# Low parts of the weights behind four attention stages made by GpSimd instead of VectorE

## The chip, the core and the metric

The kernel runs on one core of a Trainium2 chip, as one program. The metric is the device time of one execution in microseconds. Five engines work side by side, each with its own in-order queue, and meet by semaphores: TensorE (PE) multiplies matrices, VectorE (DVE) and ScalarE (ACT) work elementwise, GpSimd (POOL) is a fourth compute engine that the kernel before leaves idle, and SyncE (SP) issues the transfers of the weights.

## What is computed

Two transformer blocks over 256 tokens of width 2048, in float32, batch 1. The first has a sliding-window attention with grouped keys, relative bias and sinks, a gated linear attention in chunks of 64, gates, and a SwiGLU feed-forward net of width 5632. The second has a short causal convolution, a latent attention (MLA, 16 heads, low-rank queries and keys, rotary part, RMS norm per head), an attention over 256 memory tokens, three gates and an output product. Cut to what matters here:

```python
u = rmsnorm(h); proj = u @ w_in                      # 2048 x 8720, then split
ya = sliding_window_attention(qa, ka, va, sinks, rel_bias) @ w_proj_a
ob = gated_linear_attention(qb, kb, vb, log_a)
merged = sigmoid(gate_a) * ya + sigmoid(gate_b) * ((rmsnorm(ob) * silu(ob_gate)) @ w_proj_b)
h = h + merged @ w_out; h = h + (silu(z @ w_gate) * (z @ w_up)) @ w_down; x = rmsnorm(h)
# second block
proj = rms_norm(x) @ w_in_2                          # then split
q = rms_norm(c_q) @ w_uq; kv = rms_norm(c_kv) @ w_ukv    # per head: norm, rope, softmax, product
merged = sigmoid(g_conv)*o_conv + sigmoid(g_mla)*o_mla + sigmoid(g_mem)*o_mem
x = x + merged @ w_o
```

Nearly all the arithmetic is activations (256 rows) times weights; all weights are read once, 460 MB.

## The kernel before

A product of float32 values is made of three matmuls in a reduced float32 format (fp32r): each operand x is held as a high part (x rounded to fp32r) and a low part (x minus that), and the product is hi*hi + hi*lo + lo*hi.

The weights stream in granules of at most 1024 columns on 128 partitions (two blocks of 128 rows by 512 columns as a rule). `segments()` lists all chunks in the one order in which every engine walks them; `ALL` is the flat list. 866 granules go through two rings: `raw` with RAW = 8 slots and `w_hi`/`w_lo` with SPL = 4 slots. Per granule:

- SP loads a raw slot (L386), after `lo_done` shows that its last content was used up (the wait stands right before it).
- ACT makes the high part with a copy (L963), after the transfer landed and after TensorE used the ring slot (`w_used`), and increments `hi_done`.
- DVE makes the low part by a subtraction (L1270) after `hi_done`, and increments `lo_done`.
- PE waits for `lo_done` and runs 12 matmuls of 512 columns (L437 to L439), then increments `w_used`.

ACT and DVE also do everything else: norms, softmax, gates, copies out of PSUM. The order on each engine is written out by hand. A class `Walk`, one instance for ACT and one for DVE, keeps count and issues splits (high parts on ACT, low parts on DVE) at chosen places: `ahead(n)` issues n; `split_next`, `some` and `more` issue those of the next chunk; `background(...)` with `back(k)` serves the attention stages.

In an attention stage PE alternates between a "unit" (a group of small matmuls or transposes into a PSUM bank, `unit(fill)`, which waits for `unit_src` from DVE) and `back(k)`, k granules of a background chunk. While PE works on these, DVE and ACT prepare the next unit. `W.back(k)` on ACT and DVE first fills the ring to four granules ahead and then goes on with the attention's own instructions; so on DVE the low parts stand in line before them. ACT's counterpart runs its high parts at the same places of its own queue, each as soon as PE frees a slot, and waits for `act_req` only before its exponentials.

The four stages and what streams behind them: the window attention (`qb, kb, vb, vb, glow, ob, ob`), the gated linear attention (three each of `gate_a, proj_a`), the attention over the memory (`ge`, 4 chunks), and MLA, a loop of 2 turns with 4 pairs of heads each. A pair runs `uq` and `ukv`, its own products, and behind its attention `mz` (even pairs) or `gc` and `conv_out` (odd pairs). In a pair DVE copies the two results out of PSUM (L2140, L2147, L2150), runs `W.back`, then the norm chain: 12 sums of squares (L1284), `rsqrt` as 11 dependent instructions on 12 columns (L1290 to L1299), the scaled queries (L2172, releases the first unit), the rotary part (L2179, L2090 to L2098, released at L2184), the scaled keys (L2189). In the memory stage the like chain ends at L1958 and L1961. Both chains work from SBUF to SBUF.

Of the kernel before, what the change touches and what calls it, by code (L numbers as in the profile page):

```python
# [29 lines left out]
ALU = mybir.AluOpType  # L30
# [56 lines left out]

GRAN = 1024
RAW, SPL = 8, 4
BIASW = 384  # L90


# [22 lines left out]
def bias_constants():  # L115

    dist = 255 - np.arange(BIASW)
    d = np.maximum(dist, 0)
# [3 lines left out]
    onehot = ((np.arange(NB)[:, None] == bucket[None, :]) & seen[None, :]).astype(np.float32)  # L122
    mask = np.broadcast_to(np.where(seen, 0.0, NEG).astype(np.float32), (AH, BIASW))
    return onehot, np.ascontiguousarray(mask)
# [6 lines left out]
class Count:  # L131
# [10 lines left out]
    def next(self, by=1):  # L142
        self.n += by
        return self.at()
# [24 lines left out]
def need(eng, sem, value):  # L169

    if isinstance(value, int) and value <= 0:
        return
    eng.wait_ge(sem, value)
# [73 lines left out]
def build(nc, ap, out, scratch):  # L247
    SEG = segments()
    ALL = [(c, k) for _, n, cs in SEG for k in range(n) for c in cs]

    with ExitStack() as ctx:
        def sb(name, shape, dt=F32):
            return ctx.enter_context(nc.sbuf_tensor(name, shape, dt))

        def sem(name):
            return ctx.enter_context(nc.semaphore(name))


        raw = sb("raw", [P, RAW, GRAN])
        w_hi = sb("w_hi", [P, SPL, GRAN], F32R)  # L260
        w_lo = sb("w_lo", [P, SPL, GRAN], F32R)
        w_hi32 = w_hi[:].bitcast(F32)
# [22 lines left out]
        def area(kb, nkb):  # L285
            return arena[:, int(kb * 256):int((kb + nkb) * 256)]
# [6 lines left out]
        qb = area(30, 4).rearrange("p (t n) -> p t n", t=T)  # L293
        kb = area(34, 4).rearrange("p (t n) -> p t n", t=T)
        vb = area(38, 8).rearrange("p (t n) -> p t n", t=T)
        ob = area(46, 8).rearrange("p (t n) -> p t n", t=T)
# [10 lines left out]
        gtmp = work[:, 0:1024].rearrange("p (t n) -> p t n", t=T)  # L307
        bias_row = work[0:AH, 0:BIASW]
        onehot = work[0:NB, 512:512 + BIASW]
        rel_b = work[0:NB, 1024:1024 + AH]  # L310
        bmask = work[0:AH, 1536:1536 + BIASW]
        merged1 = area(22, 16).rearrange("p (k t n) -> p k t n", k=4, t=T)
# [35 lines left out]


        landed = [sem(f"landed{i}") for i in range(RAW)]  # L350
        hi_done, lo_done = sem("hi_done"), sem("lo_done")
        w_used = sem("w_used")
        acc_free = sem("acc_free")
        unit_src, unit_done, unit_free = sem("unit_src"), sem("unit_done"), sem("unit_free")
# [10 lines left out]
        block = ctx.enter_context(nc.Block())  # L365

        def weight_src(c, g, i):
            w = ap[c.weight]
            col = c.col if c.step == 0 else c.col + i * c.step
            v = w.rearrange("(k p) n -> p k n", p=P)[:, g * c.per:(g + 1) * c.per, :]  # L370
            return v[:, :, bass.ds(col, c.w)]


        @block.sync
        def _(sp):
            sp.dma_start(xres[:], ap["x"].rearrange("(t p) n -> p t n", p=P)).then_inc(x_in, 16)
            G = Count()
            for name, n, chunks in SEG:
                def granule(dst_size, src, shape):

                    need(sp, lo_done, G.at(1 - RAW))
                    s = G.slot(RAW)
                    dst = raw[:, s, 0:dst_size]
                    if shape > 1:
                        dst = dst.rearrange("p (k n) -> p k n", k=shape)
                    sp.dma_start(dst, src).then_inc(landed[s], 16)  # L386
                    G.n += 1

                def body(i):
                    for c in chunks:  # L390
                        if c.name == "ffn_down":
                            for k in range(8):
                                src = ap["w_ffn_down"].rearrange("(k p) n -> p k n", p=P)
                                src = src[:, bass.ds(i * 4 + k // 2, 1), (k % 2) * 1024:(k % 2 + 1) * 1024]
                                granule(GRAN, src.rearrange("p a n -> p (a n)"), 1)
                        else:
                            for g in range(c.grans):
                                granule(c.per * c.w, weight_src(c, g, i), c.per)

                if n <= 2:  # L400
                    for i in range(n):
                        body(i)
                else:
                    per = 8 if name == "ffn_down" else sum(c.grans for c in chunks)
                    with engine_loop(sp, n, {G: per}) as i:
                        body(i)
                if name == "kva":

                    sp.wait_ge(b_ready, 16)
                    shifted = bass.AP(scratch.tensor, P - 1, [[BIASW, P], [P * (BIASW + 1), AH], [1, 2 * P]])  # L410
                    sp.dma_start(bias_t, shifted).then_inc(b_ready, 16)
            for k in range(D // CW):
                sp.wait_ge(out_ready, k + 1)
                sp.dma_start(out.rearrange("(t p) n -> p t n", p=P)[:, :, k * CW:(k + 1) * CW],
                             xres[:, :, k * CW:(k + 1) * CW]).then_inc(stored, 16)
            sp.wait_ge(stored, 16 * (D // CW))
# [3 lines left out]
        def _(pe):  # L420
            G, C, U, XS = Count(), Count(), Count(), Count()
            mm = pe.matmul

            def granule(c, g, bank, banks_of=None):

                pe.wait_ge(lo_done, G.at(1))
                s = G.slot(SPL)
                per, w = c.per, c.w
                hi = w_hi[:, s, 0:per * w].rearrange("p (k n) -> p k n", k=per)
                lo = w_lo[:, s, 0:per * w].rearrange("p (k n) -> p k n", k=per)  # L430
                for k in range(per):
                    kt = g * per + k
                    for t in range(T):
                        xh = XH[c.x][:, c.x0 + kt, t * P:(t + 1) * P]
                        xl = XL[c.x][:, c.x0 + kt, t * P:(t + 1) * P]
                        o = acc[bank][:, t, 0:w]
                        mm(o, xh, hi[:, k, :], start=(kt == 0), stop=False)  # L437
                        mm(o, xh, lo[:, k, :], start=False, stop=False)  # L438
                        last = mm(o, xl, hi[:, k, :], start=False, stop=(kt == c.kts - 1))  # L439
                last.then_inc(w_used, 1)  # L440
                G.n += 1
# [220 lines left out]
            n, chunks = next((n, cc) for nm, n, cc in SEG if nm == "ffn_up")  # L662
# [18 lines left out]
            def down(first, last_pass):  # L681
                for k in range(4):

                    if k == 0:
                        XS.n += 1
                        pe.wait_ge(x_split, XS.at(0))
                    for half in range(2):
                        pe.wait_ge(lo_done, G.at(1))
                        s = G.slot(SPL)
                        for t in range(T):  # L690
                            xh = XH["A"][:, par4(k), t * P:(t + 1) * P]
                            xl = XL["A"][:, par4(k), t * P:(t + 1) * P]
                            for q in range(2):
                                o = DG[t * 4 + half * 2 + q]
                                a, z = w_hi[:, s, q * 512:(q + 1) * 512], w_lo[:, s, q * 512:(q + 1) * 512]
                                f = first and k == 0
                                e = last_pass and k == 3
                                mm(o, xh, a, start=f, stop=False, skip_group_check=True)  # L698
                                mm(o, xh, z, start=False, stop=False, skip_group_check=True)  # L699
                                last = mm(o, xl, a, start=False, stop=e, skip_group_check=True)  # L700
                        last.then_inc(w_used, 1)
                        G.n += 1
# [3 lines left out]
            def par4(k):  # L706
                return par[0] * 4 + k
            down(True, False)
            par[0] = 1
            down(False, False)  # L710
# [79 lines left out]
            n, chunks = next((n, cc) for nm, n, cc in SEG if nm == "mla")  # L790
# [466 lines left out]
            plain(4)  # L1257


        @block.vector  # L1260
        def _(dve):
            W = Walk(dve)
# [3 lines left out]

            def split(n):
                s, r = W.G.slot(SPL), W.G.slot(RAW)
                dve.wait_ge(hi_done, W.G.at(1))
                dve.tensor_tensor(w_lo[:, s, 0:n], raw[:, r, 0:n], w_hi32[:, s, 0:n], ALU.subtract).then_inc(lo_done, 1)  # L1270
                W.G.n += 1
            W.split = split

# [552 lines left out]
            n = FF // CW  # L1826
# [475 lines left out]
```

## Time and profile before

| | us |
|---|---|
| runs, median of three (lowest, highest) | 2821.07 (2819.31, 2821.19) |
| the profiled execution | 2820.21 |
| its span from first to last instruction | 2818.4 |
| PE busy | 2639.2 (94%) |
| DVE busy | 1618.3 (57%) |
| ACT busy | 1067.8 (38%) |
| POOL busy | 0.2 (0%) |

A row of the windows gives for a stretch of the span the busy time of each engine with its instructions, then the granted clock of TensorE as a share of full speed, the busy share of the DMA engines and GB/s. A row of the waits gives who waited, at which line, for which engine and line, the sum in us, how often, and the longest. A row of the timeline gives the start and length in us, engine, line, instruction, what it writes and reads, and in brackets the idle time before it with what ended it; rows with x2 or x4 are instructions in succession, merged. The ends of matmuls are modelled, and they overlap, so a gap between two matmuls reads a little shorter than it is.

### The profile page before, as it was taken

How to read it: one execution, taken by the hardware profiler on the slowest of the kernel's cores; microseconds unless marked ns; L12 is line 12 of the kernel's file. 1: busy time of each engine (PE TensorE's matmuls, PEld its weight loads, DVE VectorE, ACT ScalarE, POOL GpSimd, SP SyncE). 2: the span in 40 equal slices, each digit the busy share in tenths (PEclk: the TensorE clock that was granted, in tenths of full speed). 3: DMA queues.
4: the chain of work that ended last, by engine and by line, in shares of the span. 5: the costliest groups of instructions: out<-in, count | busy, mean ns of one | idle time of the engine just before them, and what ended most of it. 6: DMA issues, size and time to landing. Idle time of an engine off the chain costs nothing.

```text
span 2818.4 us, 32577 instructions
## 1 busy us (share of the span) xinstructions
PE 2639.2 (94%) x11795; PEld 2158.8 (77%) x11795; DVE 1618.3 (57%) x2531; ACT 1067.8 (38%) x1245; POOL 0.2 (0%) x4
## 2 busy tenths in 40 slices
PE   5999889999999999989987899999997998999999
PEld 4778666888888888878875678788886777777887
DVE  5564555456655555555566754545666776765554
ACT  3333422444443434434443334334333332334443
POOL 0000000000000000000000000000000000000000
PEclk9998999999999999999998899999998999999999
DMA  5853434655666666645563355466543443445554
GB/s 187 220 158 113 127 119 135 194 179 194 187 188 192 182 196 188 190 158 195 192 219 120 112 164 165 145 180 190 179 153 107 151 146 126 134 148 174 190 186 138
DMA packets 235264, 466.56 MB, mean 166 GB/s; under 512 B 19035, under 2 KB 27505, under 8 KB 234498
## 3 DMA queue, kind: packets, MB, share of 16 engines
q1 hardware_dynamic: 231296, 457.89, 51.9%
q10 hardware_dynamic: 3842, 7.01, 1.3%
q8 instruction: 77, 1.26, 0.2%
q14 instruction: 49, 0.40, 0.0%
HBM read 459.60 MB, written 5.24 MB: 165 GB/s over the span
## 4 chain that ended last, share of the span: by engine, by line
PE 85%; DVE 9%; DMA 2%; issue 2%; ACT 1%; DVEq 0%; SPq 0%; ACTq 0%
PE acc L437 24%; PE acc L439 23%; PE acc L438 23%; PE banks L496 2%; DVE w_lo L1270 1%; PE acc L698 1%; PE banks L699 1%; PE acc L699 1%; PE banks L700 1%; PE acc L700 1%; PE banks L698 1%; DMA bias_rows<-work 1%; DVE etmp L1284 1%; ACT w_hi L963 1%; DMA raw<-in_w_in_dram 1%
## 5 line engine op out<-in xcount | busy, mean ns | idle before, releaser
L1270 DVE TENSOR_TENSOR w_lo<-raw,w_hi 128x1024 fp32r<-128x1024 f32 (+2 forms) x866 | 1044.6, 1218 | 919.7 <-ACT w_hi L963 897.6
L963 ACT ACTIVATE w_hi<-raw 128x1024 fp32r<-128x1024 f32 (+2 forms) x866 | 909.8, 1055 | 1425.0 <-PE acc L439 1265.6
L437 PE MATMUL acc<-w_hi,x_hi_A 128*128 128x512 f32 (+2 forms) x1824 | 730.3, 400 | 21.9 <-DVE w_lo L1270 14.3
L439 PE MATMUL acc<-w_hi,x_lo_A 128*128 128x512 f32 (+2 forms) x1824 | 716.7, 393 | 0.0
L438 PE MATMUL acc<-w_lo,x_hi_A 128*128 128x512 f32 (+2 forms) x1824 | 716.3, 393 | 0.0
L437 PE MATMUL acc<-w_hi,x_hi_B 128*128 128x512 f32 (+1 forms) x1344 | 530.7, 395 | 19.7 <-DVE w_lo L1270 15.2
L438 PE MATMUL acc<-w_lo,x_hi_B 128*128 128x512 f32 (+1 forms) x1344 | 525.6, 391 | 0.0
L439 PE MATMUL acc<-w_hi,x_lo_B 128*128 128x512 f32 (+1 forms) x1344 | 525.3, 391 | 0.0
L437 PEld LDWEIGHTS acc<-w_hi,x_hi_A 128*128 128x128 f32 x1824 | 355.1, 195 | 101.6 <-issue 17.7
L439 PEld LDWEIGHTS acc<-w_hi,x_lo_A 128*128 128x128 f32 x1824 | 354.1, 194 | 72.5
L438 PEld LDWEIGHTS acc<-w_lo,x_hi_A 128*128 128x128 f32 x1824 | 355.4, 195 | 69.2 <-issue 0.8
L437 PEld LDWEIGHTS acc<-w_hi,x_hi_B 128*128 128x128 f32 x1344 | 256.7, 191 | 73.4 <-DVE w_lo L1270 16.2
L439 PEld LDWEIGHTS acc<-w_hi,x_lo_B 128*128 128x128 f32 x1344 | 256.1, 191 | 51.4
L438 PEld LDWEIGHTS acc<-w_lo,x_hi_B 128*128 128x128 f32 x1344 | 256.5, 191 | 49.6
L496 PE MATMUL banks<-cst,stage 128*128 128x128 f32 (+1 forms) x429 | 77.7, 320 | 104.1 <-DVE stage L1375 33.7
L496 PEld LDWEIGHTS banks<-cst,stage 128*128 128x128 f32 (+1 forms) x429 | 57.5, 161 | 125.3 <-DVE stage L1375 40.3
L698 PE MATMUL acc<-w_hi,x_hi_A 128*128 128x512 f32 x176 | 69.2, 393 | 5.5 <-DVE w_lo L1270 5.5
L699 PE MATMUL acc<-w_lo,x_hi_A 128*128 128x512 f32 x176 | 68.9, 392 | 0.0
L700 PE MATMUL acc<-w_hi,x_lo_A 128*128 128x512 f32 x176 | 68.9, 392 | 0.0
L698 PE MATMUL banks<-w_hi,x_hi_A 128*128 128x512 f32 x176 | 68.9, 392 | 0.0
L699 PE MATMUL banks<-w_lo,x_hi_A 128*128 128x512 f32 x176 | 68.9, 392 | 0.0
L700 PE MATMUL banks<-w_hi,x_lo_A 128*128 128x512 f32 x176 | 68.9, 392 | 0.0
(220 smaller groups left out, 1245.3 us busy)
## 6 DMA issues: line engine op xcount, KB each, us to landing
raw<-in_w_in_dram SPq DMA_DIRECT2D x377, 512.0 KB, 3.7
raw<-in_w_ffn_gate_dram SPq DMA_DIRECT2D x88, 512.0 KB, 4.3
raw<-in_w_ffn_up_dram SPq DMA_DIRECT2D x88, 512.0 KB, 4.4
raw<-in_w_ffn_down_dram SPq DMA_DIRECT2D x88, 512.0 KB, 4.7
raw<-in_w_out_dram SPq DMA_DIRECT2D x32, 512.0 KB, 4.4
raw<-in_w_mem_kv_dram SPq DMA_DIRECT2D x32, 512.0 KB, 4.3
raw<-in_w_mla_out_dram SPq DMA_DIRECT2D x32, 512.0 KB, 4.5
raw<-in_w_o_dram SPq DMA_DIRECT2D x32, 512.0 KB, 4.5
```

Of the source, the lines that this page charges most:

```text
L437: mm(o, xh, hi[:, k, :], start=(kt == 0), stop=False)
L438: mm(o, xh, lo[:, k, :], start=False, stop=False)
L439: last = mm(o, xl, hi[:, k, :], start=False, stop=(kt == c.kts - 1))
L496: return pe.transpose(o, i, ident[0:i.shape[0], 0:i.shape[0]])
L698: mm(o, xh, a, start=f, stop=False, skip_group_check=True)
L699: mm(o, xh, z, start=False, stop=False, skip_group_check=True)
L700: last = mm(o, xl, a, start=False, stop=e, skip_group_check=True)
L963: act.activation(w_hi[:, s, 0:n], raw[:, r, 0:n], ACT.Copy).then_inc(hi_done, 1)
L1270: dve.tensor_tensor(w_lo[:, s, 0:n], raw[:, r, 0:n], w_hi32[:, s, 0:n], ALU.subtract).then_inc(lo_done, 1)
L1284: return dve.tensor_tensor_reduce(out=o, in0=a, in1=b, scale=1.0, scalar=0.0, op0=ALU.mult, op1=ALU.add, accum_out=acc_)
```

## The change

GpSimd gets a program of its own: it walks the chunk list and makes the low part of every granule whose chunk's name is in `POOL_LOW`: all chunks that stream behind the four attention stages, and with them, since they carry the same names or lie between, the fourth `gate_a` and `proj_a` and the MLA chunks `uq` and `ukv`. The DVE `split` skips these, with their wait for `hi_done`, and only counts. As two engines now finish low parts, in an order that isn't fixed, `lo_done` becomes one semaphore per ring slot; SP and PE wait for the slot's own, with the round instead of the granule's number. GpSimd's program is written out for all turns of the loops.

```diff
+POOL_LOW = ("qb", "kb", "vb", "glow", "ob", "gate_a", "proj_a", "ge", "uq", "ukv", "mz", "gc", "conv_out")
...
-        hi_done, lo_done = sem("hi_done"), sem("lo_done")
+        hi_done = sem("hi_done")
+        lo_done = [sem(f"lo_done{i}") for i in range(SPL)]
...
-                    need(sp, lo_done, G.at(1 - RAW))
+                    need(sp, lo_done[G.slot(SPL)], G.rounds(SPL, SPL - RAW))
...
-                pe.wait_ge(lo_done, G.at(1))
+                pe.wait_ge(lo_done[G.slot(SPL)], G.rounds(SPL) + 1)
...
+        @block.gpsimd
+        def _(pool):
+            G = Count()
+
+            def low(c, n):
+                s, r = G.slot(SPL), G.slot(RAW)
+                if c.name in POOL_LOW:
+                    pool.wait_ge(hi_done, G.at(1))
+                    pool.tensor_tensor(w_lo[:, s, 0:n], raw[:, r, 0:n], w_hi32[:, s, 0:n], ALU.subtract).then_inc(lo_done[s], 1)
+                G.n += 1
+
+            for name, n, chunks in SEG:
+                for _ in range(n):
+                    for c in chunks:
+                        for _ in range(8 if c.name == "ffn_down" else c.grans):
+                            low(c, c.per * c.w)
...
             def split(n):
                 s, r = W.G.slot(SPL), W.G.slot(RAW)
-                dve.wait_ge(hi_done, W.G.at(1))
-                dve.tensor_tensor(w_lo[:, s, 0:n], raw[:, r, 0:n], w_hi32[:, s, 0:n], ALU.subtract).then_inc(lo_done, 1)
+                if ALL[W.next - 1][0].name not in POOL_LOW:
+                    dve.wait_ge(hi_done, W.G.at(1))
+                    dve.tensor_tensor(w_lo[:, s, 0:n], raw[:, r, 0:n], w_hi32[:, s, 0:n], ALU.subtract).then_inc(lo_done[s], 1)
                 W.G.n += 1
```

## Rows read from the trace of the kernel before

**Rows 1.** Windows, the four attention stages in order; columns as told above.
```profile
145.00:330.00 185.00, 173.19 (x845) 142.99 (x844) 97.76 (x141) 67.73 (x120) 0.00 (x0) 0.93 0.42 127
330.00:500.00 170.00, 154.10 (x640) 113.49 (x641) 94.77 (x164) 56.39 (x61) 0.00 (x0) 0.95 0.42 132
1630.00:1850.00 220.00, 206.67 (x903) 168.49 (x902) 113.84 (x158) 82.19 (x92) 0.00 (x0) 0.97 0.53 157
2135.00:2560.00 425.00, 388.01 (x1759) 314.82 (x1758) 296.58 (x794) 143.92 (x190) 0.00 (x0) 0.96 0.44 143
```

**Rows 2.** Waits of PE in the MLA loop, 2135 to 2560 us.
```profile
PE acc L437 <- DVE w_lo L1270: 14.0, 6, 7.0
PE banks L496 <- DVEq L2184: 13.4, 8, 2.2
PE banks L496 <- DVE stage L2172: 6.1, 4, 1.6
PE banks L496 <- DVE stage L2189: 3.5, 8, 0.5
```

**Rows 3.** Waits of PE in the memory attention, 1630 to 1850 us.
```profile
PE banks L496 <- DVE stage L1961: 10.3, 4, 3.9
```

**Rows 4.** Groups: low parts, high parts, GpSimd; count | busy us, mean ns | idle.
```profile
L1270 DVE TENSOR_TENSOR w_lo<-raw,w_hi 128x1024 fp32r<-128x1024 f32 (+2 forms) x866 | 1044.6, 1218 | 919.7 <-ACT w_hi L963 897.6
L963 ACT ACTIVATE w_hi<-raw 128x1024 fp32r<-128x1024 f32 (+2 forms) x866 | 909.8, 1055 | 1425.0 <-PE acc L439 1265.6
...
L2288 POOL MEMSET const-float32-1.0<- 128x1 f32 x1 | 0.1, 99 | 0.0
```

**Rows 5.** Timeline of DVE, an even pair of the MLA loop.
```profile
2145.73 0.69 DVE L2150 COPY arena<-acc 128x512 f32<-128x512 f32 x1
2146.54 2.36 DVE L1270 TENSOR_TENSOR w_lo<-raw,w_hi 128x1024 fp32r<-128x1024 f32 x2
...
2153.68 0.87 DVE L2172 TENSOR_SCALAR stage<-arena,sm 128x128 f32<-128x128 f32 x4
```

**Rows 6.** Timeline of DVE, the odd pair after it.
```profile
2190.94 0.69 DVE L2150 COPY arena<-acc 128x512 f32<-128x512 f32 x1
...
2198.89 0.87 DVE L2172 TENSOR_SCALAR stage<-arena,sm 128x128 f32<-128x128 f32 x4
```

**Rows 7.** Timeline of ACT: first and last of four, then of five.
```profile
2145.00 1.06 ACT L963 ACTIVATE w_hi<-raw 128x1024 fp32r<-128x1024 f32 x1 [1.65 <-PE acc L439]
...
2153.16 1.06 ACT L963 ACTIVATE w_hi<-raw 128x1024 fp32r<-128x1024 f32 x1 [1.65 <-PE acc L439]
...
2190.22 1.06 ACT L963 ACTIVATE w_hi<-raw 128x1024 fp32r<-128x1024 f32 x1 [1.66 <-PE acc L439]
...
2201.10 1.06 ACT L963 ACTIVATE w_hi<-raw 128x1024 fp32r<-128x1024 f32 x1 [1.66 <-PE acc L439]
```

**Rows 8.** Timeline of PE, the odd pair's first unit.
```profile
2200.90 0.60 PE L496 MATMUL banks<-cst,stage 128*128 128x128 f32 x4
```

**Rows 9.** Timeline of DVE and PE at the MLA loop's turn.
```profile
2337.68 4.10 DVE L1270 TENSOR_TENSOR w_lo<-raw,w_hi 128x768 fp32r<-128x768 f32 x4 [3.31 <-issue]
...
2338.69 0.69 PE L437 MATMUL acc<-w_hi,x_hi_B 128*128 128x384 f32 x1 [6.97 <-DVE w_lo L1270]
```

**Rows 10.** Windows, the stretch right after that wait.
```profile
2338.70:2342.40 3.70, 3.70 (x12) 3.70 (x13) 3.07 (x3) 0.00 (x0) 0.00 (x0) 0.50 0.72 222
```

**Rows 11.** Timeline of ACT before the first pair, four high parts merged.
```profile
2123.98 3.46 ACT L963 ACTIVATE w_hi<-raw 128x768 fp32r<-128x768 f32 x4
```

**Rows 12.** Timeline of DVE before the first pair, the end of its chain.
```profile
2129.91 0.23 DVE L2125 COPY stage<-stage 128x128 f32<-128x128 f32 x1
```

**Rows 13.** Timeline of DVE and ACT in the memory attention.
```profile
1665.61 1.22 DVE L1950 COPY arena<-acc 128x1024 f32<-128x1024 f32 x1
1668.82 1.06 ACT L963 ACTIVATE w_hi<-raw 128x1024 fp32r<-128x1024 f32 x1 [1.66 <-PE acc L439]
...
1672.10 0.43 DVE L1961 COPY stage<-arena 128x512 f32<-128x512 f32 x1
```

More of the change, by code:

```diff
@@ L687, in down @@
                     for half in range(2):
-                        pe.wait_ge(lo_done, G.at(1))
+                        pe.wait_ge(lo_done[G.slot(SPL)], G.rounds(SPL) + 1)
                         s = G.slot(SPL)
```

## The prediction

> **What bounds the kernel now.** I read the table of windows first, the waits of TensorE second, the timeline last. TensorE sets the end: the profiled execution is 2818.4 us of span and 2820.2 us in all, 0.9 us under the median of the three runs (2821.07), so nothing needs scaling. In the stretches without attention TensorE is busy all the time and the change can't touch it. The four attention stages are the stretches of [rows 1]: 1000 us, with TensorE busy 922. So at most 78 us of gaps, with what the lower clock there costs, are open to a gain. In the last stage, the largest, the waits [rows 2] say whom TensorE waits for: 23 us for VectorE's norm chain (L2172, L2184, L2189) and 14 us for low parts. In the memory stage it is the same kind of chain [rows 3].
>
> Two things stand on VectorE's one queue: the low parts, 1218 ns each, and the chains of small instructions that release TensorE's next unit [rows 4]. Where VectorE is late, it is by the low parts ahead of the chain.
>
> **Removed.** By the chunk list GpSimd takes 49 granules behind the window attention, 36 + 12 at the gated one, 32 at the memory, 112 in the MLA loop: 241 of 866, some 241 x 1.2 = 290 us of VectorE. Worth on the path:
>
> 1. MLA, even pairs. After the copy L2150 VectorE makes two low parts, 2.36 us, then runs the norm chain to the end of L2172 [rows 5]. The chain's own length is 2154.55 - 2146.42 - 2.36 = 5.8 us. 2.36 us earlier would remove the wait on L2172 (1.6 of it) and 0.8 of the next: 2.3 us, x4 = 9.3.
> 2. Odd pairs: [rows 6] the same chain ends at 2199.76, TensorE comes at 2200.90 [rows 8]. It waits for the later chain steps and a late low part, about 2.4 us; all goes, x4 = 9.6.
> 3. Low parts that TensorE waits for, 14 us [rows 2], with four of about 0.7 already in step 2: 11.2. The 7.0 us one is at the loop's turn: ACT has long made the high parts, VectorE makes the low parts only at 2337.68 [rows 9]. GpSimd's list isn't a loop. Behind it TensorE has 0.50 of its clock (1.2 GHz) for 3.7 us [rows 10], so 1.9 us comes back too. Before the first pair another 1.9 us.
> 4. Memory stage: the copy of 1665.61 stands behind a high and a low part (1.06 + 1.22 [rows 4, 13]), so 2.3 us of the wait goes, twice: 4.6.
> 5. The window and gated stages: their gaps (11.8 and 15.9 us by [rows 1]) I take as short unit-to-unit latencies, not low parts. 3 us, from 0 to 8.
>
> Sum of the gains: 9.3 + 9.6 + 11.2 + 1.9 + 1.9 + 4.6 + 3 = 41.5 us.
>
> **Added: one instruction on GpSimd.** No row shows it; GpSimd's own rows are memsets of one column, 0.1 us [rows 4]. Lower bound: VectorE's 1.22 us for the same tile. Upper bound: if it fetches its two operands one after the other, two such passes, 2.44. I take 2.4. TensorE eats a granule in 2.72 us (four high parts from 2145.00 to 2153.16, three periods [rows 7]), so GpSimd keeps up, at 88% of its time. A ring of four gives a low part 3 x 2.72 = 8.2 us; it needs 1.06 + 2.4. Hidden, with 4.7 us to spare. Nothing else is queued behind its wait.
>
> The Trainium skill (GPSIMD Engine Reference, Performance versus the Vector engine) gives 4497 ns for 2048 fp32 columns of tensor_tensor; halved, an estimate of 2.25 us. The sum below would shrink by about 5 us by it.
>
> **Added: GpSimd and VectorE side by side on SBUF.** The trace has no such moment. The bounds: no effect (0), or a VectorE instruction that reads two SBUF operands can't run while GpSimd's does, so that every GpSimd instruction that falls into a norm chain lengthens it by its own 2.4 us. I take the upper end: VectorE takes both operands at one element per cycle (1218 ns for 1024 columns), so it draws two streams at once, and the change puts two more beside them. The chain is made of just such instructions (squares, the Newton steps of rsqrt, the rotation), and a small one pays as much as a large one.
>
> - Even pair: high parts end at 2146.06, 2148.8, 2151.5, 2154.2, one period apart [rows 7]. GpSimd runs 2.4 us behind each, to 2156.6. The chain starts at 2146.42, gets the three gaps of 0.3 us, and does its other 4.9 us afterwards: 2161.5 instead of 2154.55, +6.9. TensorE was already waiting there: x4 = 27.6.
> - Odd pair: five high parts, 2190.22 to 2201.10 [rows 7]; GpSimd to 2204.6. Four gaps, 1.2 us; the other 4.6 end at 2209.1. TensorE was ready at 2200.90: +8.3, a further 1.0 at the next unit, less the 0.7 low part: +8.6, x4 = 34.4. The clock falls there too, which it doesn't now: 1.9 x 4 = 7.4.
> - Before the first pair the four high parts end by 2127.4 and the chain ends at 2129.91 + 0.23 [rows 11, 12]. Four low parts (two of 768 columns) hold it for some 7 us; less the 1.9 us low-part wait: +5.2.
> - Memory stage: three GpSimd instructions until 2 x 1.2 past the high part of 1668.82 [rows 13], 1672.3. The chain of 5.7 us (1666.8 to 1672.5) has 0.7 in gaps, ends at 1677.3: +4.8, x2 = 9.6.
> - Window and gated stages: there ScalarE makes its high parts before the softmax and after it, so GpSimd is mostly idle during the chain: 0 (-3 to +8).
> - What stays of the gains: the low parts at pair ends and the loop's turn, 11.2 + 1.9 = 13.1.
>
> Net: 27.6 + 34.4 + 7.4 + 5.2 + 9.6 - 13.1 = +71. 2820.2 + 71 = **2891 us**.
>
> The Trainium skill (SBUF — State Buffer, Who interferes with whom) says that a VectorE instruction with two SBUF inputs and a GpSimd instruction that reads SBUF share a port as an exclusive lock, and the second to start blocks fully. No trace here shows it; by it the sum is the one above, without it the 2779 below. The rule speaks against this change.
>
> **A semaphore per slot.** As many waits and increments as before on SP and TensorE; in loops the waited value is again a register. GpSimd reads the raw slot 1.2 us longer than VectorE; the transfers are eight granules, 21.8 us, ahead. Nothing. Without that lead each late transfer would cost its delay.
>
> **Rivals.**
> A. *No interference.* The 41.5 us come whole: 2820.2 - 41.5 = 2779 us. For it: all waits of [rows 2] are on VectorE. Against it: two operand streams at once on each.
> B. *Partial.* VectorE gets in first, or only some forms collide; the low parts then come late but within the ring's 4.7 us. Half the gain is lost again: about 2800 us.
> C. *GpSimd's rate.* From 2.72 us per instruction on, it is the bound of every uninterrupted stretch. At 3.0 us, 0.28 x 241 = 67 us against the 41.5 gained: 2846 us. Against it: 2.4 by the bound.
> D. *It does nothing to the path*: the chains stay as they are because the waits are for ScalarE: within 0.2%. [rows 3] with a low part ahead of the chain speaks against it.
>
> **How the numbers follow.** Forecast 0.51, A 0.27, B 0.11, C 0.07, D 0.04. A measurement of this kernel tells 0.2% (5.6 us) from no change. Slower: 0.51 + 0.07 and 0.01 of B = 0.59. Same: 0.04 + 0.01 = 0.05. Faster: 0.36. The range reaches down to 2772, into A with a little more gained; up to 2915, the forecast with 12 instead of 8 stalls of 8 us or 2.7 us instructions. The forecast's own range is 2850 to 2915.
>
> **What would show it.** GpSimd busy some 241 x 2.4 = 580 us, one instruction per 2.7 us in a run. VectorE's L1270 at 625. If the forecast holds: in the MLA loop the twelve-column steps L1295 to L1299 lie 2.4 us apart in places, not 0.2, or are that long; TensorE's waits on L2172 grow from 6 to over 60 us, those for L1270 vanish; 3 us at 0.50 of the clock behind each. If A: L2172 waits are gone and the steps keep their 0.2 us. If C: TensorE waits for the GpSimd line in the middle of chunks. Wrong altogether if GpSimd's instruction is under 1.5 us, or if TensorE waits in places where now it is always busy.

## The result and the profile after

| | us |
|---|---|
| before, on the same chip, median of 4 runs (lowest, highest) | 2820.19 (2818.02, 2821.19) |
| after, median of 4 runs (lowest, highest) | 2887.10 (2884.04, 2887.60) |
| ratio after to before, 95% interval | 1.0236 [1.0218, 1.0254] |
| the profiled execution of after, its span | 2887.03, 2885.2 |

The changed kernel is 67 us slower; the forecast was 71 us slower. In the code of after the low part is L1270 on GpSimd and L1291 on VectorE. L2172, L2184, L2189, L1961 and L2125 of before are L2193, L2205, L2210, L1982 and L2146, and the sum of squares L1284 is L1305.

The page, busy time of each engine, with its instructions:

```profile
PE 2647.0 (92%) x11795; PEld 2165.0 (75%) x11795; DVE 1449.6 (50%) x2290; ACT 1066.9 (37%) x1245; POOL 565.5 (20%) x245
```

VectorE lost 169 us of work, GpSimd took over 565 us. TensorE, which sets the end, is idle for 59 us more (2885.2 - 2647.0 = 238.2, before 2818.4 - 2639.2 = 179.2) and busy for 7.8 us more with the same matmuls, by its clock. The groups of instructions by line, of after (the last figures are the idle time before them):

```profile
L1291 DVE TENSOR_TENSOR w_lo<-raw,w_hi 128x1024 fp32r<-128x1024 f32 x625 | 762.2, 1225 | 787.7 <-ACT w_hi L965 777.5
L1270 POOL TENSOR_TENSOR w_lo<-raw,w_hi 128x1024 fp32r<-128x1024 f32 (+1 forms) x241 | 565.3, 2357 | 2031.0 <-ACT w_hi L965 2030.2
L1305 DVE CUSTOM_DVE_ANT_0 work<-arena 128x128 f32<-128x128 f32 (+1 forms) x96 | 95.4, 1057 | 0.3
```

The third is the sum of squares of MLA's norm chain. Before, the same 96 instructions, beside an idle GpSimd:

```profile
L1284 DVE CUSTOM_DVE_ANT_0 work<-arena 128x128 f32<-128x128 f32 (+1 forms) x96 | 18.8, 262 | 0.0
```

So 96 instructions of 0.26 us became 96 of 1.06 us in the mean: 76.6 us more in a group that nobody changed. By the trace of after, 36 of the 96 start while a GpSimd instruction is under way. All 36 end 0.15 us after that instruction does; the other 60 run at their own length. The waits of TensorE in the whole span of after answer to [rows 2, 3]:

```profile
PE banks L498 <- DVE stage L2193: 58.8, 8, 7.6
PE banks L498 <- DVE stage L1982: 18.3, 4, 8.1
PE banks L498 <- DVE stage L2146: 15.2, 1, 15.2
PE banks L498 <- DVEq L2205: 13.8, 8, 1.7
PE acc L439 <- DVE w_lo L1291: 13.2, 3, 6.4
```

The wait on the scaled queries went from 6.1 us in four places to 58.8 us in all eight pairs. The wait for the memory stage's chain went from 10.3 us to 18.3. The timeline of the first even pair of after (start, length) shows how. Copied are GpSimd's instructions, the held ones of VectorE with the two free ones of the first gap, and the unit that TensorE waits for:

```profile
2160.53 0.69 DVE L2171 COPY arena<-acc 128x512 f32<-128x512 f32 x1
2160.95 2.39 POOL L1270 TENSOR_TENSOR w_lo<-raw,w_hi 128x1024 fp32r<-128x1024 f32 x1 [0.33 <-ACT w_hi L965]
2161.26 2.23 DVE L1305 CUSTOM_DVE_ANT_0 work<-arena 128x128 f32<-128x128 f32 x1
2163.42 0.21 DVE L1305 CUSTOM_DVE_ANT_0 work<-arena 128x64 f32<-128x64 f32 x1
2163.57 0.28 DVE L1305 CUSTOM_DVE_ANT_0 work<-arena 128x128 f32<-128x128 f32 x1
2163.66 2.45 POOL L1270 TENSOR_TENSOR w_lo<-raw,w_hi 128x1024 fp32r<-128x1024 f32 x1 [0.33 <-ACT w_hi L965]
2163.78 2.48 DVE L1305 CUSTOM_DVE_ANT_0 work<-arena 128x128 f32<-128x128 f32 x1
2166.38 2.47 POOL L1270 TENSOR_TENSOR w_lo<-raw,w_hi 128x1024 fp32r<-128x1024 f32 x1 [0.27 <-ACT w_hi L965]
2166.55 2.45 DVE L1305 CUSTOM_DVE_ANT_0 work<-arena 128x128 f32<-128x128 f32 x1
2169.10 2.46 POOL L1270 TENSOR_TENSOR w_lo<-raw,w_hi 128x1024 fp32r<-128x1024 f32 x1 [0.24 <-ACT w_hi L965]
2169.29 2.41 DVE L1305 CUSTOM_DVE_ANT_0 work<-arena 128x128 f32<-128x128 f32 x1
...
2174.57 0.87 DVE L2193 TENSOR_SCALAR stage<-arena,sm 128x128 f32<-128x128 f32 x4
...
2175.58 0.68 PE L498 MATMUL banks<-cst,stage 128*128 128x128 f32 x2 [7.65 <-DVE stage L2193]
```

Read the pairs of rows together. The square of 2161.26 ends at 2163.49, just after GpSimd's instruction (2160.95 + 2.39 = 2163.34). Two more pass in 0.21 and 0.28 us in GpSimd's gap. The one of 2163.78 starts after the next GpSimd instruction did and is held to its end, and so are those of 2166.55 and 2169.29: four in all. The chain runs from 2161.26 to 2175.44, 14.2 us; its own length is 5.8 us. The stretches of [rows 1] in after (length, busy time of PE, PEld, DVE, ACT and POOL, then PEclk, DMA share, GB/s):

```profile
145.00:330.00 185.00, 174.94 (x857) 144.76 (x855) 47.48 (x97) 69.06 (x120) 104.29 (x45) 0.92 0.45 130
330.00:500.00 170.00, 153.06 (x643) 113.24 (x644) 49.22 (x122) 55.80 (x62) 100.16 (x42) 0.96 0.44 133
1630.00:1855.00 225.00, 203.75 (x894) 166.98 (x893) 87.48 (x123) 81.47 (x92) 76.72 (x32) 0.95 0.51 152
2145.00:2610.00 465.00, 382.53 (x1698) 308.71 (x1698) 248.77 (x680) 137.81 (x184) 251.50 (x108) 0.90 0.40 119
```

TensorE's idle time in them is 10.1, 16.9, 21.3 and 82.5 us, before 11.8, 15.9, 13.3 and 37.0. The first two stages, where GpSimd is busy for 204 us too, hardly moved; MLA did, and its granted clock fell from 0.96 to 0.90. In those two stages five VectorE instructions are over 0.2 us longer than their like before, 3.4 us in all; in the memory stage six, 13.0 us; from 2100 us on 43, 89.6 us.

### The profile page after: what moved, and what is told of

The parts are those of the page before. It is cut to its first block, busy times and chain, and to the rows that moved or that the text cites. A ratio compares the mean times of both kernels' runs of the same rounds, so it can differ in the third digit from the quotient of the medians.

```text
span 2885.2 us, 32087 instructions
## 1 busy us (share of the span) xinstructions
PE 2647.0 (92%) x11795; PEld 2165.0 (75%) x11795; DVE 1449.6 (50%) x2290; ACT 1066.9 (37%) x1245; POOL 565.5 (20%) x245
## 4 chain that ended last, share of the span: by engine, by line
PE 83%; DVE 11%; issue 2%; DMA 2%; ACT 2%; DVEq 0%; SPq 0%; POOL 0%; ACTq 0%
PE acc L439 23%; PE acc L441 23%; PE acc L440 23%; DVE work L1305 3%; PE banks L498 2%; DVE etmp L1305 2%; PE acc L700 1%; PE acc L702 1%; PE acc L701 1%; PE banks L701 1%; PE banks L702 1%; PE banks L700 1%; DMA bias_rows<-work 1%; DMA raw<-in_w_in_dram 1%; ACT w_hi L965 1%
## 5 line engine op out<-in xcount | busy, mean ns | idle before, releaser
L1291 DVE TENSOR_TENSOR w_lo<-raw,w_hi 128x1024 fp32r<-128x1024 f32 x625 | 762.2, 1225 | 787.7 <-ACT w_hi L965 777.5
L1270 POOL TENSOR_TENSOR w_lo<-raw,w_hi 128x1024 fp32r<-128x1024 f32 (+1 forms) x241 | 565.3, 2357 | 2031.0 <-ACT w_hi L965 2030.2
L498 PE MATMUL banks<-cst,stage 128*128 128x128 f32 (+1 forms) x429 | 86.1, 346 | 172.6 <-DVE stage L2193 58.8
L1305 DVE CUSTOM_DVE_ANT_0 work<-arena 128x128 f32<-128x128 f32 (+1 forms) x96 | 95.4, 1057 | 0.3
```

Source lines behind the costliest of these rows:

```text
L498: return pe.transpose(o, i, ident[0:i.shape[0], 0:i.shape[0]])
L1270: pool.tensor_tensor(w_lo[:, s, 0:n], raw[:, r, 0:n], w_hi32[:, s, 0:n], ALU.subtract).then_inc(lo_done[s], 1)
L1305: return dve.tensor_tensor_reduce(out=o, in0=a, in1=b, scale=1.0, scalar=0.0, op0=ALU.mult, op1=ALU.add, accum_out=acc_)
```

## The experiments

The theory: GpSimd's subtraction and a VectorE instruction with its operands in SBUF exclude each other, and each GpSimd instruction that falls into a norm chain costs the chain about its own length. The rivals: the new semaphores or GpSimd's work as such cost the time; the low parts come too late; any work of GpSimd, a write too, does it.

### Which part of the change costs

`e1_slots_only` keeps the semaphore per slot and gives all low parts back to VectorE; `e2_first_two` gives GpSimd those of the window and the gated stage alone (97 granules), `e3_mla_only` those of the MLA loop alone (112).

```diff
-POOL_LOW = ("qb", "kb", "vb", "glow", "ob", "gate_a", "proj_a", "ge", "uq", "ukv", "mz", "gc", "conv_out")
+POOL_LOW = ()                                                      # e1_slots_only
+POOL_LOW = ("qb", "kb", "vb", "glow", "ob", "gate_a", "proj_a")    # e2_first_two
+POOL_LOW = ("uq", "ukv", "mz", "gc", "conv_out")                   # e3_mla_only
```

> The semaphores per ring slot alone: the list of chunks for GpSimd is empty, VectorE makes all 866 low parts. Collision (a GpSimd instruction holds back VectorE's instructions that work from SBUF to SBUF): the slots cost nothing, 2820 us, within 3 us of the kernel before. Rival, the new semaphores and their register values cost time in the loops: some of the 67 us stay, 2830 us or more.

> GpSimd makes the low parts of the first two attention stages alone (97 granules), as in the change. Collision: there ScalarE's high parts mostly don't fall into VectorE's chains, and the trace of after is only 0.9 us later at their end: 2819 to 2823 us. Rival, a low part that takes 2.36 us instead of 1.22 keeps TensorE waiting wherever it is used: 97 x 1.14 us would be up to 110 us if it were all on the path, at least some 20 us: 2840 us or more.

> GpSimd makes the low parts of the MLA chunks alone (112 granules). By the traces the loop is 52 us longer and the stretch before its first pair 6.5 us: collision says 2820 + 59 = 2879 us, with the waits on the scaled queries near 59 us. If the loss came from all 241 instructions alike, it would be 112/241 of 67: 2851 us.

Measured, against 2819.02 us before on that chip: e1 2818.58 (ratio 0.9998 [0.9989, 1.0008]), e2 2820.91 (1.0006 [0.9996, 1.0015]), e3 2878.27 (1.0209 [1.0192, 1.0226]). The semaphores cost nothing. 97 GpSimd instructions of the same length cost 1.9 us, within the noise, where they hold only five instructions of VectorE, for 3.4 us in all. MLA alone costs 59.3 us of the 67, and its page repeats the waits of after:

```profile
PE banks L498 <- DVE stage L2193: 58.8, 8, 7.7
```

### The same work at another time

`e6_gated` leaves all 241 low parts on GpSimd, but GpSimd waits at eleven places (before the first pair, in each of the eight pairs, twice in the memory stage) until VectorE's chain is through.

```diff
+                dve.sem_inc(calm, 1)        # VectorE, after the staging copy that ends a chain
...
+                                if pair == 8:       # GpSimd: behind uq and ukv of each pair
+                                    calms += 1
+                                    pool.wait_ge(calm, calms)
                                 low(c, c.per * c.w)
```

> All 241 low parts on GpSimd as in the change, but it waits on a new semaphore at eleven places (once before the first pair, once in each of the eight pairs, once in each half of the memory attention) until VectorE's norm chain is through, so that the same instructions run later. Collision: the waits on the scaled queries fall from 59 to under 10 us, TensorE waits about 1.2 us per pair for the first low part after the chain, and the stall at the loop's turn stays gone: 2815 to 2830 us. Rival, GpSimd's low parts are simply late: made still later they cost more, 2890 us or above.

Measured: 2814.59 us, 0.9983 [0.9974, 0.9993]. Groups by line of this kernel:

```profile
L1327 DVE CUSTOM_DVE_ANT_0 work<-arena 128x128 f32<-128x128 f32 (+1 forms) x96 | 34.7, 424 | 0.3
L1276 POOL TENSOR_TENSOR w_lo<-raw,w_hi 128x1024 fp32r<-128x1024 f32 (+1 forms) x241 | 561.7, 2353 | 1961.2 <-ACT w_hi L966 1563.2 <-DVEq L2172 309.4 <-DVEq L2238 76.5
```

GpSimd does as many instructions as in after, as long as there, and 72.5 us are gone. So neither its total work nor its rate is what costs, but where its instructions fall. The squares are not quite free yet: they take 15.9 us more than before in all, some 2 us per pair, since the chain of a pair begins while a GpSimd instruction is under way and its first square is held to the end of that. Little is left of the 41.5 us that rival A had counted. One cause is that GpSimd now starts late after each chain; in the MLA stretch TensorE waits for it:

```profile
PE acc L440 <- POOL w_lo L1276: 8.5, 5, 1.8
```

### What of the instruction collides

Four kernels change the GpSimd instruction alone. In `e4_write_only`, `e5_one_read` and `e11_write_long` the low parts of the 241 granules are zero: the products of those granules miss their hi\*lo term, with TensorE's work as it was.

```diff
-pool.tensor_tensor(w_lo[:, s, 0:n], raw[:, r, 0:n], w_hi32[:, s, 0:n], ALU.subtract).then_inc(lo_done[s], 1)
+pool.memset(w_lo[:, s, 0:n].bitcast(F32), 0.0).then_inc(lo_done[s], 1)                          # e4_write_only
+pool.tensor_scalar(w_lo[:, s, 0:n], raw[:, r, 0:n], 0.0, None, ALU.mult).then_inc(lo_done[s], 1)  # e5_one_read
```

> As the change, but GpSimd writes zeros over the low parts (a memset of the same tile) instead of computing them: the 241 products with low parts are left out of the result, every wait stays. GpSimd then reads nothing from SBUF. If the collision is on reading, VectorE's sums of squares are back at 0.26 us each and only the scaling instructions (L2193, from SBUF to SBUF at 0.2 us per 128 columns) may be held: 2775 to 2800 us. If any GpSimd instruction on SBUF holds VectorE back, each for its own length: the sums of squares stay long, in proportion to the memset's duration, e.g. 2820 us or more at 1 us each.

> As the change, but GpSimd makes the low part as raw times zero: one operand read instead of two, again zeros. Duration between half and all of 2.36 us. If every reading GpSimd instruction holds VectorE back for its whole length, the chain grows by that length times three to five: about 2820 to 2860 us, in proportion; if only GpSimd's second operand collides with VectorE's, the chains keep the length of before: 2780 us.

Measured, against 2820.03: e4 2774.03 us, 0.9843 [0.9827, 0.9859]; e5 2832.54, 1.0049 [1.0032, 1.0066]. The groups by line, of e4 and then of e5:

```profile
L1270 POOL MEMSET w_lo<- 128x1024 f32 (+1 forms) x241 | 226.3, 940 | 2255.5 <-ACT w_hi L965 2255.5
L1305 DVE CUSTOM_DVE_ANT_0 work<-arena 128x128 f32<-128x128 f32 (+1 forms) x96 | 18.9, 263 | 0.3
L2187 DVE TENSOR_SCALAR sm<-sm 128x4 f32<-128x4 f32 x8 | 7.7, 964 | 0.3
```

```profile
L1270 POOL TENSOR_SCALAR w_lo<-raw 128x1024 fp32r<-128x1024 f32 (+1 forms) x241 | 651.9, 2730 | 1889.0 <-ACT w_hi L965 1889.0
L1305 DVE CUSTOM_DVE_ANT_0 work<-arena 128x128 f32<-128x128 f32 (+1 forms) x96 | 26.5, 340 | 0.3
```

With writes alone the squares are back at 263 ns and the time is within 5 us of rival A's 2779. That it comes so near is in part luck. By the start times of the same high parts, e4 gains 7 us in the window and gated stages (A counted 3), 9.9 in the memory stage (4.6) and 27 in the MLA stretch (33.9), and its GpSimd instruction, 0.94 us, is shorter than VectorE's 1.22, which A's was not. VectorE is held mainly at one place: the TENSOR_SCALAR of four columns takes 964 ns, 170 before, which is a memset's length. e5 gave neither of the two times that stood against each other. Its GpSimd instruction is longer than the subtraction and as long as a granule of TensorE (2.72 us), yet the longest square is 1.18 us and the mean 340 ns. All 96 squares start while a GpSimd instruction is under way. The nine that start within 0.3 us of its start are held, and end 1.14 to 1.19 us after it; the 87 that start later than 1.0 us after it run at their own length. So this instruction with one SBUF operand holds the squares for the first 1.2 us of its 2.73, not to its end. Why is open.

`e10_halves` makes the same subtraction in two instructions of half the columns. `e11_write_long` writes each low part 2¼ times, about as long as the subtraction, and reads nothing: it is meant to separate "too late" from "colliding".

```diff
-pool.tensor_tensor(w_lo[:, s, 0:n], raw[:, r, 0:n], w_hi32[:, s, 0:n], ALU.subtract).then_inc(lo_done[s], 1)
+for h in range(2):                                                   # e10_halves
+    ins = pool.tensor_tensor(w_lo[:, s, h * n // 2:(h + 1) * n // 2], raw[:, r, h * n // 2:(h + 1) * n // 2],
+                             w_hi32[:, s, h * n // 2:(h + 1) * n // 2], ALU.subtract)
+ins.then_inc(lo_done[s], 1)
...
+for part in (n, n):                                                  # e11_write_long
+    pool.memset(wide[:, 0:part], 0.0).then_inc(again, 1)
+    writes.n += 1
+    pool.wait_ge(again, writes.n)
+pool.memset(wide[:, 0:n // 4], 0.0).then_inc(lo_done[s], 1)
```

> As the change, but each low part on GpSimd is made by two instructions of half the columns (1.2 us each). If VectorE's held instruction waits for the end of the one GpSimd instruction under way, the held sums of squares shrink from about 2.4 to about 1.3 us each and twice as many are held, while GpSimd's total in a chain stays: 2880 to 2895 us. If GpSimd only takes the shared path when both its halves are free, or VectorE gets priority at the seam, the chain gets shorter: under 2865 us.

> As the write-only kernel, but the zeros are written two and a quarter times, one after the other, so that GpSimd is as long at each low part as in the change (about 2.3 us) and still reads nothing; the products with these 241 low parts are left out. If duration by itself is hidden by the ring of four: 2774 to 2785 us, as with 0.94 us. If the lateness of GpSimd's low parts were a part of the loss: 2800 us or more.

Measured, against 2820.28: e10 2881.26 us, 1.0217 [1.02, 1.0234]; e11 2804.12, 0.9944 [0.9927, 0.9961]. Of e10, groups by line:

```profile
L1271 POOL TENSOR_TENSOR w_lo<-raw,w_hi 128x512 fp32r<-128x512 f32 (+1 forms) x482 | 605.0, 1285 | 1986.3 <-ACT w_hi L965 1983.4
L1308 DVE CUSTOM_DVE_ANT_0 work<-arena 128x128 f32<-128x128 f32 (+1 forms) x96 | 86.1, 959 | 0.3
```

Halves hold 64 squares instead of 36, each for about half as long; the longest is 1.37 us. The loss is GpSimd's busy time inside the chain, whether it comes in whole or in half instructions. Of e11:

```profile
L1274 POOL MEMSET w_lo<- 128x1024 f32 (+1 forms) x482 | 453.7, 941 | 1971.8 <-ACT w_hi L966 1957.7
L1312 DVE CUSTOM_DVE_ANT_0 work<-arena 128x128 f32<-128x128 f32 (+1 forms) x96 | 18.9, 263 | 0.3
L2217 DVE TENSOR_SCALAR stage<-arena,sm 128x128 f32<-128x128 f32 x32 | 12.2, 629 | 1.4
L2194 DVE TENSOR_SCALAR sm<-sm 128x4 f32<-128x4 f32 x8 | 7.8, 969 | 0.3
```

The expected time was missed by some 20 us, and 2804 us lies where the expectation had put lateness as a part of the loss. It can't be the main part: low parts about as late as GpSimd's subtraction makes them leave the kernel 16 us faster than before, not 67 us slower, and the squares run free. But writing has a collision of its own: TENSOR_SCALAR from SBUF to SBUF is held (L2217 629 ns, 280 before; L2194 969, 170 before; with four more such lines 23.5 us of VectorE in all). How much of the 30 us between e4 and e11 is this collision and how much is lateness, no run separates. The Trainium skill (SBUF — State Buffer, Who interferes with whom) says that on a shared port pair VectorE's two-input instructions contend with a GpSimd instruction that reads SBUF and not with one that only writes, while copy, cast and tensor_scalar can use both ports of a kind and so contend as well, and that the second to start waits for the whole of the first. The traces agree for the two-input subtraction (held up to 2.48 us beside 2.45), for the memset beside the squares (263 ns) and beside TENSOR_SCALAR. They do not agree for e5, whose reading instruction held a square for 1.18 us at the most.

### Is there a way to the gain

`e7_lead3` is the kernel before with one number changed: in VectorE's turn of an MLA pair, three granules are made ahead instead of two, so that one low part instead of two stands in line before the chain.

```diff
-                W.background(len(others), False, 2)
+                W.background(len(others), False, 3)
```

> The kernel before with one low part per MLA pair moved on VectorE alone: three instead of two go ahead of the copy of keys and values, where VectorE idles 2 us, so one fewer (1.2 us) stands ahead of the norm chain. No GpSimd. If the chain's start sets TensorE's waits there, 8 x 1.2 us = 9 to 10 us faster: 2809 to 2812 us. If not, 2819 us.

Measured: 2808.88 us, 0.9957 [0.994, 0.9974]. `e8_uq_ukv` leaves VectorE's order as it was before and gives GpSimd only `uq` and `ukv`, 32 granules; GpSimd waits for the chain ahead of the first pair.

```diff
-POOL_LOW = ("qb", "kb", "vb", "glow", "ob", "gate_a", "proj_a", "ge", "uq", "ukv", "mz", "gc", "conv_out")
+POOL_LOW = ("uq", "ukv")
...
+                        if c.name == "uq" and first_uq:
+                            pool.wait_ge(calm, 1)
```

> GpSimd makes the low parts of uq and ukv alone, 32 granules, the first four after the chain before the loop; VectorE's order is the one of before. Only the low parts TensorE waited for at pair ends and at the loop's turn are won: 11.2 + 1.9 - 0.6 = 12 us faster, 2807 us. Rival, they collide with other work of VectorE there: 2815 us or more.

Measured: 2819.22 us, 0.9997 [0.9988, 1.0007], which is the rival's time. GpSimd met no chain, but behind the odd pairs it met a long VectorE instruction. Timeline of e8, first odd pair:

```profile
2234.74 2.40 POOL L1271 TENSOR_TENSOR w_lo<-raw,w_hi 128x1024 fp32r<-128x1024 f32 x1 [0.33 <-ACT w_hi L966]
2234.97 3.25 DVE L1506 TENSOR_TENSOR arena<-arena 128x1024 f32 x1
```

L1506 adds two SBUF tiles; it takes 1.22 us alone and 3.25 us here: it starts 0.23 us after GpSimd does and ends 1.1 us after it. It is held so behind three of the four odd pairs. That this took the gain is not shown: `e9_best` below has the same three held additions and is faster. By the same high parts in the traces of before and e8, the loop's turn is 6.7 us shorter (8.9 were counted) and the eight pairs are 6.7 us longer together, 5.0 of it in TensorE's busy time, which is its clock. The wait of 4.2 us at the end of the loop, which the expectation had counted as won, stayed; its low part is VectorE's.

`e9_best` is e8 with the 3 of e7, and with the memory stage's low part moved behind its chain on VectorE. `e12_no_pool` is the same order on VectorE without any work for GpSimd.

```diff
-                W.split_next()
+                W.ahead(W.head(W.next - 1, None) - W.part)
+                W.next, W.part = W.next + 1, 0
+                W.ahead(3)
...
-                W.background(2)
-                W.back(2)
                 rsqrt(4, ED)
...
+                    if hh == 0:
+                        W.ahead(1)
+                        W.background(2)
+                        W.back(2)
```

> e7's order; GpSimd makes only the low parts of uq and ukv (32 granules, whose high parts come between the chains), the first four after the chain before the loop; and in the memory attention the low part ahead of the copy moves behind the chain. Expected: 9.6 for e7, 11.2 + 1.9 for the low parts TensorE waits for, 4.6 for the memory stage, less 0.6 for the first pair: 27 us faster, 2792 us. If those GpSimd instructions still meet chains, under 15 us faster.

> The fastest version so far without GpSimd: only VectorE's low parts are moved (three ahead of the copy of keys and values in an MLA pair; in the memory attention the one ahead of the copy goes behind the chain). By e7 (11 us) and the memory stage (4.6 us): 2804 us, so that GpSimd's 32 low parts in the fastest version were worth 11 us. If GpSimd's part of it was nothing, as in the run with uq and ukv alone: 2794 us.

Measured: e9 2793.47 us, 0.9907 [0.989, 0.9923], the fastest that computes everything; e12 2798.69, 0.993 [0.9916, 0.9943], between the two times that were expected. e9 met its forecast of 2792 with other terms: the memory stage gave 7.2 us where 4.6 were counted, and the 4.2 us at the end of the loop stayed. Of the 27 us that e9 gains, about 21 come from the order on VectorE and about 6 from GpSimd; the intervals of these two overlap, so GpSimd's share is not settled. The stretch at the loop's turn is 7.0 us shorter in e9 and unchanged in e12. TensorE's waits for low parts in the whole span, of e9 and then of e12, point the same way:

```profile
PE acc L440 <- DVE w_lo L1296: 21.0, 8, 6.4
```

```profile
PE acc L437 <- DVE w_lo L1270: 29.4, 10, 6.7
```

## Why the prediction was right

The step that decided, that a two-operand instruction of VectorE waits for GpSimd's whole one, held, and so did its price. Term by term, measured by the start times of the same high parts on ScalarE in both traces:

| term | predicted, us | measured, us |
|---|---|---|
| window and gated stages, and on to the memory stage | 0 | +1.1 |
| memory stage | +9.6 | +7.0 |
| before the first pair | +5.2 | +6.7 |
| four even pairs | +27.6 | +24.9 |
| four odd pairs (34.4 + 7.4 for the clock) | +41.8 | +34.4 |
| gains that stay | -13.1 | -7.2 |
| sum | +71 | +66.9 |

The number is nearer than its terms: 4 us off in all, with errors of up to 7 us that partly cancel. The forecast had a chance of 0.51, and the whole range that was given, 2772 to 2915 us, reaches to both sides of no change, so that the time alone proves little; the held squares and the experiments carry the mechanism.

- **GpSimd's instruction.** Predicted 2.4 us, measured 2.40 for 1024 columns (2.36 over all 241). It keeps TensorE's pace: TensorE waits for it once, 5.9 us at 118 us of the span, where before it had waited 4.7 us for VectorE. The page's rows of GpSimd are called rough, but here start to start and the length agree (2160.95 to 2163.66 with 0.33 idle).
- **Even pairs.** Predicted +6.9, so a wait of 8.5 us on L2193; measured 7.65 in the first. The mis-sized term is what passes in GpSimd's gap: counted at 0.3 us of chain work, it is three squares per period, 0.57 us by their start times before (twelve from 2148.82 to 2151.10). The chain took 14.2 us instead of 15.1.
- **Odd pairs.** Predicted a wait of 8.3 us, measured 7.1, and the further 1.0 at the next unit was 0.6 (L2205 1.73 us, before 1.17). TensorE's idle time grew by 6.7 us per odd pair, where 8.6 was counted. The eight stalls together are 58.8 us where the terms meant 67.
- **Clock.** Predicted 7.4 us for the odd pairs, as four times 1.9; TensorE's busy time grew by 7.5 us in them, but as 2.95, 2.51, 1.23 and 0.85. Two errors cancel here. Each stall costs more than 1.9 us where the clock was full before, and behind the last two odd pairs it was not, against what the prediction says. Windows of before, behind the first and the third odd pair (columns as above):

```profile
2206.00:2209.00 3.00, 3.00 (x15) 2.47 (x14) 2.99 (x4) 0.97 (x1) 0.00 (x0) 1.00 0.87 241
2411.00:2414.00 3.00, 3.00 (x9) 2.33 (x8) 3.00 (x4) 0.00 (x0) 0.00 (x0) 0.50 0.88 223
```

  In the MLA stretch the granted clock is 0.90 in the mean, 0.96 before, and behind the stall of the first even pair, in which TensorE had been idle for 7.65 us, it is at 1.2 GHz. A window of after:

```profile
2176.00:2180.00 4.00, 1.99 (x9) 1.20 (x8) 3.75 (x19) 0.00 (x0) 0.00 (x0) 0.50 0.00 0
```

- **Gains that stay.** Predicted 13.1, measured 7.2. Of the 11.2 us of low-part waits the one at the loop's turn went (7.0, of which 1.6 stay as a wait for nothing that the profile shows), and the clock behind it gave 1.8 back, as counted (1.9). The one of 4.2 us is that of `gm` at the end of the loop, whose low part is still VectorE's: counted as gone, it stayed. This error and those of the pairs are of opposite sign. The row of after:

```profile
PE acc L439 <- DVE w_lo L1291: 4.2, 1, 4.2
```

- **Window and gated stages.** Zero, as predicted (-0.4 us from 101 to 500 us; +1.6 us comes from 500 to 1600, where GpSimd makes no low part), and e2 shows it for GpSimd's 97 instructions there.
- **The signs.** GpSimd busy 565 us (about 580 expected), 625 low parts on VectorE, the wait on the scaled queries from 6.1 to 58.8 (over 60 expected). Wrong was which instructions would be held: not the twelve-column steps of rsqrt but the squares ahead of them. In the timeline of after the steps of rsqrt, from 2172.31 on, lie 0.2 us apart, since GpSimd's last instruction of the pair had ended at 2171.56. The price was the same, as it hangs on GpSimd's time in the chain and not on who is held.
- **Rivals.** A's 2779 is near what e4 measured (2774), but only by a GpSimd that reads nothing, and with other terms. B's picture, some forms collide and others don't, is right for one-operand and writing instructions (e5, e11), not for the subtraction. C fell with 2.40 us and e6. D fell with 67 us.

One part of the argument rests on the experiments only in part: that the 41.5 us of gains would have come whole without a collision. e4 gives 46, with a shorter instruction; e11, about as long as the subtraction, gives 16, with the collision of its writes.

## What to carry to other kernels

Before giving GpSimd work that reads two SBUF tiles, look at what VectorE runs from SBUF meanwhile: a chain that TensorE waits for pays nearly the whole GpSimd time that falls into it, however small its instructions are, and cutting GpSimd's instructions in half brought at most 6 us (e10). Work of the same kind was free in stretches where it held VectorE for 3.4 us in all (e2), and a wait that keeps it out of the chain gives the loss back (e6). First see whether the order on the busy engine's own queue can be changed: making one low part earlier in each MLA pair and one later in each half of the memory stage brought 21 of the 27 us of the best version with GpSimd (e12 against e9).

## What the runs showed of the hardware that was not expected

- Instructions of two columns are held like large ones, and TENSOR_SCALAR too, which has one SBUF tile as input. Timeline of after, before the first pair; the four low parts of GpSimd are merged in one row:

```profile
2133.03 8.17 POOL L1270 TENSOR_TENSOR w_lo<-raw,w_hi 128x768 fp32r<-128x768 f32 x4 [304.95 <-ACT w_hi L965]
...
2136.73 2.20 DVE L1311 TENSOR_SCALAR sm<-sm 128x2 f32<-128x2 f32 x1
2138.96 2.26 DVE L1313 TENSOR_SCALAR sm<-sm 128x2 int32<-128x2 int32 x1
...
2145.41 0.69 PE L498 MATMUL banks<-cst,stage 128*128 128x128 f32 x2 [15.20 <-DVE stage L2146]
```

- On GpSimd a multiplication of one tile by a constant (128x1024, float32 to fp32r) takes 2.78 us (e5), longer than the subtraction of two tiles, 2.40 us (after). A memset takes 0.96 us (e4).
- That longer instruction holds the squares for less: no longer than 1.19 us after its start, where the subtraction holds them to its end (the longest square is 1.18 us in e5, 2.48 us in after).
- A memset of GpSimd doesn't hold the squares (263 ns) but holds a TENSOR_SCALAR of four columns from SBUF to SBUF, which then takes 0.96 us.
